# Two blocks on one core: the seven-product stage's weight places at 256 instead of 320 bytes, and `t2` ahead of `to` in the second attention's schedule

## The chip, the cores and the metric

One core of a Trainium2 chip. The time is the device time of one execution in microseconds (us), the median of three runs. Engines: PE (matmuls; PEld is its row of weight loads), DVE (vector), ACT (scalar), POOL, and SP, which here only issues DMAs.

## The reference, cut to what matters

A block with a mixer (a convolution branch and an attention with a forget gate) and a SwiGLU feed-forward, and then a differential attention layer; the last layer of the second block has no part in the result, since one layer of the list is run. All in fp32, with 512 tokens and width 1024.

```python
def swiglu(h, w_gate_up, w_down):
    gu = jnp.einsum("bsd,df->bsf", h, w_gate_up)     # 1024 x 5632
    g, u = jnp.split(gu, 2, axis=-1)
    return jnp.einsum("bsf,fd->bsd", jax.nn.silu(g) * u, w_down)

def diff_attention_layer(x, norm_g, w_in, ...):
    q, k, v, z = jnp.split(rms_norm(x, norm_g) @ w_in, 4, axis=-1)
    ...                                              # 16 heads, two maps of 64 each
    weights = probs[:, :, 0] - lam * probs[:, :, 1]
    o = einsum(weights, v)                           # causal, blocks of 128 queries
    o = rms_norm(o, head_norm_g) * (1.0 - lam_0)
    return x + (o.reshape(b, s, BRANCH) * jax.nn.silu(z)) @ w_out
```

## The kernel before

**Products in three parts.** Every fp32 operand x is kept as two fp32r tiles, high part and rest (`hth`/`htl` for the activations, `whi`/`wlo` for weights, `pth`/`ptl` for attention weights). ACT writes the high part by a copy (its helper `copy` is line 1291), DVE the rest by a subtraction (helper `lower`, line 1609). A product is three matmuls: high x high, high x rest, rest x high. The function `three` (lines 927 to 929, and 932 to 934 where weights are the stationary operand) writes them.

**One list of steps.** `Order` writes a list `STEPS` of named steps. Each engine walks the whole list and emits its own part of each step, so the order of the list is the order on PE, DVE, ACT and POOL alike; semaphores hold them together. `merge` deals out the steps of a projection of the next group (`proj2`) between those of the attention of the present pair of heads (`pair`), one `yield` at a time. `bank()` takes the next of four spare PSUM banks in turn, and PE's `claim` waits until the bank's last reader is done.

**The seven-product stage.** The gate and up projections (`gp` steps, blocks j = 1 to 10; block 0 is computed directly by `three`, steps `gu`) multiply 2 x 2 blocks by seven products instead of eight, with 256 tokens as moving operand. Each of the 70 products takes eight k-and-column pieces of three matmuls (L1162, L1164, L1165), 128 x 128 stationary by 256 columns. Their weights stand in four places of 1024 elements in `whi_all` and `wlo_all`, tiles of 4096 + 256 elements:

```python
SHIFT = 80                               # elements of 4 bytes
s = (first_slot + BLOCK(j, p)) % 4
c = SHIFT + 1024 * ((s + 2) % 4)
cs = slice(256 * kt + P * fb, 256 * kt + P * fb + P)   # inside the place; P = 128
```

The program puts `whi` at byte 44032 of a partition, `wlo` at 61440, and `hth`, `htl` and the other matmul operands of these stages also at multiples of 512. The weights of `three` start at multiples of 128 elements in these tiles, so on multiples of 512 bytes; those of the stage start 320 bytes past one. One further stationary operand is off that grid: `wf2`, which the step `fm` uses (L1014 and L1015, 16 columns of 4 bytes for each k from 0 to 7, 512 tokens moving), lies at byte 221152, which is 480 past a multiple of 512; its slice for k starts 64 k bytes further.

**The second attention's pair schedule.** For a pair of heads `even` and `odd`: `s2` computes scores, DVE takes maxima, ACT exponentials, `cb` combines the two maps, `t2` transposes the attention weights (three parts of up to four 128 x 128 tiles, L1230) and ACT and DVE copy them out as `pth2` and `ptl2` (shown as `pth` and `ptl`), `p2` multiplies them with v (L1243 to L1245, four key blocks, the third and fourth need part 2 of `t2`). `ga`/`gb` make the norm of a head. `to` transposes the gated norm of a head (L1261); DVE multiplies it with the head's result into `ots` (L1985), and ACT waits for that and sends `ots` to DRAM (L1585; for heads below 12), from where SP loads it back four heads at a time. POOL has no part in `to` or `t2`.

Of the kernel before, what the change touches and what calls it, by code (L numbers as in the profile page):

```python
# [172 lines left out]
class Order:  # L173
# [27 lines left out]
    def put(self, *step):  # L201
        self.steps.append(step)
# [42 lines left out]
    def bank(self):  # L245
        self.turns += 1
        return self.spare[self.turns % len(self.spare)]
# [312 lines left out]
    def pair(self, even):  # L560
        put, bank, odd, past = self.put, self.bank, even + 1, even > 0
        self.scores(even, 0)
        self.scores(even, 1)
        yield
        if past:
            put("t2", even - 1, 0, bank())
        put("cb", even, 0)
        put("ab", odd)
        yield
        if past:  # L570
            self.second_tiles(even - 1)
            put("t2", even - 1, 2, bank())
        put("cb", even, 1)
        yield
        self.scores(even, 2)
        self.scores(odd, 0)
        yield
        put("cb", even, 2)
        yield
        if past:  # L580
            put("to", even - 2, bank())
        put("cb", even, 3)
        yield
        put("cb", odd, 0)
        put("ab", odd + 1)
        yield
        if past:
            put("p2", even - 1, bank())
        put("cb", odd, 1)
        yield  # L590
        put("t2", even, 0, bank())
        yield
        self.second_tiles(even)
        yield
        self.scores(odd, 1)
        self.scores(odd, 2)
        yield
        if past:
            put("to", even - 1, bank())
        put("t2", even, 2, bank())  # L600
        put("cb", odd, 2)
        yield
        put("p2", even, bank())
        put("cb", odd, 3)
        yield
        yield
# [35 lines left out]
def build(nc, A, out, x1_d, x2_d, ot_d):  # L642
# [10 lines left out]
    with ExitStack() as ctx:  # L653
# [194 lines left out]
        BANK = lambda j, p: RING[(5 * (j - 1) + BANKS[p]) % 8]  # L848
        first_slot = 2 * (1 - H[W.mix + 1].slot)
        assert first_slot == 0  # L850
        SHIFT = 80
        p1_t, sg0_t, u2_t, u3_t, c22_t, c21_t = (tf[0][:, 0:512], tf[0][:, 512:1024], tf[1][:, 0:512],
                                                 tf[1][:, 512:1024], xf[0][:, 0:512], xf[0][:, 512:1024])
        moving = [(lambda k: (hth[:, k, 0:256], htl[:, k, 0:256])), (lambda k: (sh[2][:, k, :], sl[2][:, k, :])),
# [6 lines left out]
        def slot_of(j, p):  # L861
            s = (first_slot + BLOCK(j, p)) % 4
            c = SHIFT + 1024 * ((s + 2) % 4)
            cs = slice(c, c + 1024)
# [740 lines left out]
        def _(e):  # L1605
# [32 lines left out]
            for s in STEPS:  # L1638
# [234 lines left out]
                elif kind == "gx":  # L1873
                    j, p = a
                    o = ps[BANK(j, p)][:, :]
                    if p == 3:
                        dve.wait_ge(snap_a, j)
                        dve.wait_ge(mm, PRODUCT(j, 3))
                        e.tensor_tensor(u2_t, o, p1_t, ALU.add).then_inc(comb_d, 1)
                        dve.wait_ge(comb_d, COMB(j, U2))  # L1880
                        e.tensor_tensor(u3_t, ps[BANK(j, 1)][:, :], u2_t, ALU.add).then_inc(comb_d, 1)
                    elif p == 4:
                        dve.wait_ge(comb_d, COMB(j, U3))
                        dve.wait_ge(mm, PRODUCT(j, 4))
                        e.tensor_tensor(c22_t, o, u3_t, ALU.add).then_inc(comb_d, 1)
                    elif p == 5:
                        dve.wait_ge(mm, PRODUCT(j, 5))
                        e.tensor_tensor(c21_t, u3_t, o, ALU.subtract).then_inc(comb_d, 1)
                    elif p == 6:
                        dve.wait_ge(sg1_a, j)  # L1890
                        dve.wait_ge(comb_d, COMB(j, C22))
                        e.tensor_tensor(gu[:, 2 * j:2 * j + 2, 256:512], pair(c21_t), pair(c22_t),
                                        ALU.mult).then_inc(comb_d, 1)
                        dve.wait_ge(mm, PRODUCT(j, 6))
                        e.tensor_tensor(u2_t, o, u2_t, ALU.add).then_inc(comb_d, 1)
                        dve.wait_ge(comb_d, COMB(j, C12))
                        dve.wait_ge(sg0_a, j)
                        e.tensor_tensor(gu[:, 2 * j:2 * j + 2, 0:256], pair(sg0_t), pair(u2_t),
                                        ALU.mult).then_inc(comb_d, 1)
# [293 lines left out]
```

## Time and profile before

| | |
|---|---|
| median of 3 runs | 1282.76 us (1282.42 to 1284.1) |
| the profiled execution | 1282.49 us, of which the span from first to last instruction is 1280.8 us |
| PE busy | 1274.0 us of the span |
| DVE, ACT, POOL busy | 795.0, 611.6, 298.4 us |
| granted TensorE clock | 1.00 of 2.4 GHz over the whole span |
| seven-product stage | 392 to 590 us |
| second attention with its projections | about 729 to 1163 us |

In the views, a row has a start and a length in us, engine, line of the kernel, output and inputs. Matmuls are pipelined: their lengths overlap, and the pace is the distance between starts. Idle time in brackets is that of the row's engine ahead of it.

### The profile page before, as it was taken

The page shows a single profiled execution, that of the slowest core. Times are in us where ns is not written, and L with a number is a line of the kernel's source. Part 1 is how long each engine was busy: PE and PEld are TensorE (multiplying, and loading weights), DVE is VectorE, ACT ScalarE, POOL GpSimd, SP SyncE. Part 2 cuts the span into 40 slices and gives each one's busy share as a digit, 9 for nine tenths or more (in the row PEclk, how much of TensorE's full clock was granted, in tenths as well). Part 3 has the DMA queues.
Part 4 walks back from the last instruction along what each step waited for, and adds up shares of the span by engine and source line. Part 5 has one row for each costly group of instructions (what it writes and reads, how often), then busy time and mean ns, then how long its engine had stood idle before and what let it go on. Part 6 is the DMA issues. An engine that isn't in the chain of part 4 may idle for free.

```text
span 1280.8 us, 18355 instructions
## 1 busy us (share of the span) xinstructions
PE 1274.0 (99%) x7170; PEld 1085.6 (85%) x7170; DVE 795.0 (62%) x1578; ACT 611.6 (48%) x1300; POOL 298.4 (23%) x203
## 2 busy tenths in 40 slices
PE   9999999999999999999999999999999999999999
PEld 6788888888899999999888888888888888887787
DVE  5435665443479987877333647676767667677743
ACT  5336654333445444445233445565556555556531
POOL 2023310000055656540001412131312223131110
PEclk9999999999999999999999999999999999999999
DMA  6322232333533334243226322222222222223511
GB/s 235 108 58 75 59 99 71 96 98 99 205 124 105 105 121 132 67 132 115 82 99 218 112 66 84 82 74 74 83 71 98 88 75 75 74 81 123 184 59 66
DMA packets 110441, 130.35 MB, mean 102 GB/s; under 512 B 7569, under 2 KB 87697, under 8 KB 110354
## 3 DMA queue, kind: packets, MB, share of 16 engines
q1 hardware_dynamic: 104594, 112.39, 27.2%
q10 hardware_dynamic: 5760, 16.78, 3.6%
q8 instruction: 57, 0.93, 0.3%
q14 instruction: 30, 0.25, 0.1%
HBM read 119.72 MB, written 9.44 MB: 101 GB/s over the span
## 4 chain that ended last, share of the span: by engine, by line
PE 98%; DVE 1%; ACT 0%; DMA 0%; POOL 0%; issue 0%; SPq 0%; ACTq 0%
PE ps L927 17%; PE ps L929 16%; PE ps L928 16%; PE ps L932 7%; PE ps L934 7%; PE ps L933 7%; PE ps L1164 5%; PE ps L1165 5%; PE ps L1162 5%; PE ps L1220 3%; PE ps L1230 1%; PE ps L1202 1%; PE ps L1254 1%; PE ps L1244 1%; PE ps L1245 1%; PE ps L1243 1%
## 5 line engine op out<-in xcount | busy, mean ns | idle before, releaser
L1609 DVE TENSOR_TENSOR wlo<-raw,whi 128x512 fp32r<-128x512 f32 (+1 forms) x294 | 233.7, 821 | 187.2 <-ACT whi L1291 186.5
L1291 ACT ACTIVATE whi<-raw 128x512 fp32r<-128x512 f32 (+2 forms) x338 | 208.5, 649 | 117.9 <-PE ps L929 84.5
L927 PE MATMUL ps<-whi,hth 128*128 128x512 f32 x592 | 242.3, 409 | 0.2 <-DVE wlo L1609 0.2
L929 PE MATMUL ps<-wlo,hth 128*128 128x512 f32 x592 | 231.5, 391 | 0.0
L928 PE MATMUL ps<-whi,htl 128*128 128x512 f32 x592 | 231.2, 390 | 0.0
L2043 POOL TENSOR_TENSOR wlo<-raw,whi 128x384 fp32r<-128x384 f32 (+1 forms) x44 | 49.2, 1135 | 416.6 <-ACT whi L1291 416.6
L927 PEld LDWEIGHTS ps<-whi,hth 128*128 128x128 f32 x592 | 111.3, 188 | 26.4 <-issue 5.2
L929 PEld LDWEIGHTS ps<-wlo,hth 128*128 128x128 f32 x592 | 111.1, 188 | 24.7
L928 PEld LDWEIGHTS ps<-whi,htl 128*128 128x128 f32 x592 | 111.6, 188 | 19.2
L932 PE MATMUL ps<-hth,whi 128*128 128x512 f32 (+1 forms) x288 | 111.5, 387 | 0.0
L934 PE MATMUL ps<-hth,wlo 128*128 128x512 f32 (+1 forms) x288 | 108.9, 378 | 0.0
L933 PE MATMUL ps<-htl,whi 128*128 128x512 f32 (+1 forms) x288 | 108.9, 378 | 0.0
L1559 ACT ACTIVATE px<-px,nm 128x128 f32<-128x128 f32 (+3 forms) x128 | 70.4, 551 | 54.4 <-DVE nm L1949 54.4
L1165 PE MATMUL ps<-sh,wlo 128*128 128x256 f32 x320 | 89.9, 281 | 0.0
L1162 PE MATMUL ps<-sh,whi 128*128 128x256 f32 x320 | 89.9, 281 | 0.0
L1164 PE MATMUL ps<-sl,whi 128*128 128x256 f32 x320 | 89.9, 281 | 0.0
L2012 POOL TENSOR_TENSOR rq<-rq,neghalf 128x8 f32<-128x8 f32 x32 | 52.4, 1638 | 123.1 <-DVE rq L1912 123.1
L2102 POOL TENSOR_TENSOR hn<-hn,neghalf 128x4 f32<-128x4 f32 x16 | 16.8, 1051 | 247.5 <-DVE hn L1976 247.5
L1291 ACT ACTIVATE px<-px,rl 128x128 f32<-128x128 f32 (+1 forms) x64 | 36.0, 562 | 78.8 <-DVE rl L1962 78.8
L1609 DVE TENSOR_TENSOR wlo<-ts,whi 128x1024 fp32r<-128x1024 f32 x40 | 66.5, 1684 | 4.1 <-ACT whi L1291 4.1
L2081 POOL TENSOR_TENSOR ts<-raw 128x1024 f32<-128x1024 f32 x20 | 58.3, 2916 | 40.0 <-DVE wlo L1609 38.6
L1162 PE MATMUL ps<-hth,whi 128*128 128x256 f32 x240 | 67.4, 281 | 0.0
(362 smaller groups left out, 2913.9 us busy)
## 6 DMA issues: line engine op xcount, KB each, us to landing
raw<-in_l_w_in SPq DMA_DIRECT2D x64, 512.0 KB, 4.4
raw<-in_w_gate_up SPq DMA_DIRECT2D x44, 512.0 KB, 4.7
raw<-in_w_in SPq DMA_DIRECT2D x13, 1024.0 KB, 5.2
raw<-in_w_down SPq DMA_DIRECT2D x10, 1024.0 KB, 4.9
raw<-in_l_w_out SPq DMA_DIRECT2D x8, 1024.0 KB, 5.0
raw<-in_w_in SPq DMA_DIRECT2D x26, 256.0 KB, 3.5
raw<-in_w_branch SPq DMA_DIRECT2D x8, 512.0 KB, 3.9
raw<-in_w_out SPq DMA_DIRECT2D x4, 1024.0 KB, 4.9
```

The source lines that it names most:

```text
L927: e.matmul(o, ah, wh[:, cs], start=a, stop=False)
L928: e.matmul(o, al, wh[:, cs], start=False, stop=False)
L929: m = e.matmul(o, ah, wl[:, cs], start=False, stop=z)
L932: e.matmul(o, wh[:, cs], ah, start=a, stop=False)
L933: e.matmul(o, wh[:, cs], al, start=False, stop=False)
L934: m = e.matmul(o, wl[:, cs], ah, start=False, stop=z)
L1162: e.matmul(o, wh[:, cs], ah, start=q == 0 and kt == 0 and p not in (2, 6), stop=False, skip_group_check=True)
L1164: e.matmul(o, wh[:, cs], al, start=False, stop=False, skip_group_check=True)
L1165: m = e.matmul(o, wl[:, cs], ah, start=False, stop=z, skip_group_check=True)
L1291: return e.activation(out, in_, ACT.Copy, **how)
L1559: e.activation(sl, sl, ACT.Exp, bias=nm2[:, c:c + 1], scale=-1.0, accum_out=ls2[:, c:c + 1]).then_inc(exp2_a, 1)
L1609: return e.tensor_tensor(out, src, hi_part.bitcast(F32), ALU.subtract)
```

## The change

The weight places of the seven-product stage start at 64 elements (256 bytes) instead of 80 (320 bytes) past the start of the tile; sizes, order and waits stay as they are. In `pair`, for pairs after the first, the step `t2` (part 2 of head even) comes ahead of `to` (head even-1) in the list, on every engine; as `bank()` is called in the new order, the two also trade spare banks. For the first pair nothing changes.

```diff
@@ pair
         self.scores(odd, 2)
         yield
         if past:
+            put("t2", even, 2, bank())
             put("to", even - 1, bank())
-        put("t2", even, 2, bank())
+        else:
+            put("t2", even, 2, bank())
         put("cb", odd, 2)
         yield
         put("p2", even, bank())
@@ build
-        SHIFT = 80
+        SHIFT = 64
```

## Rows read from the trace of the kernel before

**Rows 1.** The page's busy line, and the table by stage (seven products; second attention).

```profile
PE 1274.0 (99%) x7170; PEld 1085.6 (85%) x7170; DVE 795.0 (62%) x1578; ACT 611.6 (48%) x1300; POOL 298.4 (23%) x203
...
core 0: us, PE busy (x) PEld busy (x) DVE busy (x) ACT busy (x) POOL busy (x), PEclk, DMA share, GB/s
392.00:590.00 198.00, 198.00 (x1684) 198.00 (x1683) 164.96 (x146) 92.36 (x106) 108.03 (x37) 1.00 0.34 107
729.00:1163.00 434.00, 433.98 (x2334) 357.40 (x2334) 295.74 (x781) 245.40 (x617) 99.63 (x70) 1.00 0.24 80
```

**Rows 2.** PE's waits from 20 us on, with total, times and longest.

```profile
PE ps L1243 <- DVE ptl L1609: 0.9, 1, 0.9
```

**Rows 3.** Weight loads by line: duration min/median/max in ns, first and last start.

```profile
L1162 PEld LDWEIGHTS ps<-sh,whi x320: 192/192/192, 395.0 to 589.6; 128*128 128x128 f32 x160
...
L1164 PEld LDWEIGHTS ps<-sl,whi x320: 187/188/188, 395.1 to 589.8; 128*128 128x128 f32 x160
...
L933 PEld LDWEIGHTS ps<-htl,whi x18: 192/192/192, 380.0 to 391.9; 128*128 128x128 f32 x18
```

**Rows 4.** Timeline of PE at the stage's start: start, length, instruction.

```profile
391.53 0.28 PE L932 MATMUL ps<-hth,whi 128*128 128x256 f32 x1
...
391.89 0.28 PE L932 MATMUL ps<-hth,whi 128*128 128x256 f32 x1
...
392.25 0.28 PE L1162 MATMUL ps<-hth,whi 128*128 128x256 f32 x1
```

**Rows 5.** Timeline of PE, the last L1162 of 560.

```profile
589.76 0.28 PE L1162 MATMUL ps<-sh,whi 128*128 128x256 f32 x1
```

**Rows 6.** Timeline of PE, `fm`: k = 0, 1, 2, and the matmul after its last.

```profile
59.17 0.39 PE L1014 MATMUL ps<-hth,wf 128*16 128x512 f32 x1
...
59.62 0.40 PE L1014 MATMUL ps<-hth,wf 128*16 128x512 f32 x1
...
60.09 0.39 PE L1014 MATMUL ps<-hth,wf 128*16 128x512 f32 x1
...
62.85 0.39 PE L932 MATMUL ps<-hth,whi 128*128 128x512 f32 x1
```

**Rows 7.** Timeline of the last pair's step with `to` and `t2`, PE and ACT.

```profile
1160.44 0.60 PE L1261 MATMUL ps<-ident,og 128*128 128x128 f32 x4
...
1160.88 0.49 PE L1230 MATMUL ps<-ident,px 128*128 128x128 f32 x3
...
1162.72 0.36 ACT L1551 ACTIVATE zs<-ps 128x256 f32<-128x256 f32 x1
```

**Rows 8.** Timeline of PE, the last pair's `p2` of head 12, and what follows.

```profile
1163.93 0.39 PE L1243 MATMUL ps<-pth,v2h 128*128 128x512 f32 x1
...
1166.21 0.39 PE L1243 MATMUL ps<-pth,v2h 128*128 128x256 f32 x1 [0.92 <-DVE ptl L1609]
...
1166.85 0.28 PE L1245 MATMUL ps<-ptl,v2h 128*128 128x128 f32 x1
1166.96 0.45 PE L927 MATMUL ps<-whi,hth 128*128 128x512 f32 x1
```

**Rows 9.** The chain that ended last, there: start, length, what.

```profile
1163.69 0.33 DVE zs L1934
...
1164.71 0.33 ACTq L1585
...
1165.08 0.50 ACT pth L1291
...
1165.60 0.57 DVE ptl L1609
```

**Rows 10.** Timeline of PE, an undisturbed `p2`: first and third block, and what follows.

```profile
1142.01 0.39 PE L1243 MATMUL ps<-pth,v2h 128*128 128x512 f32 x1
...
1143.21 0.29 PE L1243 MATMUL ps<-pth,v2h 128*128 128x256 f32 x1
...
1143.87 0.44 PE L927 MATMUL ps<-whi,hth 128*128 128x512 f32 x1
```

**Rows 11.** Timeline of SP's queue: the read-back of heads 8 to 11.

```profile
1169.01 0.37 SPq L2127 DMA_DIRECT2D raw<-ot_dram  x1
```

## The prediction

> **What bounds the kernel now.** First the busy line of the page and the table by stage [rows 1]: PE is busy 1274.0 of 1280.8 us, the granted clock is 1.00 (the 2.4 GHz level) in both big stages, and DVE, ACT and the DMAs have room. So the span is the number of matmuls times their pace, and an edit is worth something only if it changes a pace or one of the few waits of PE. Then the list of PE's waits: after the first 20 us PE waited once for another engine, 0.9 us for `ptl` [rows 2]. Busy time hides the pace, though: a 256-column matmul lasts 0.28 us [rows 4], yet 1680 of them fit into 198 us. The pace is the distance between starts, so the timeline of PE comes next.
>
> **Part one, the place.** L1162, L1164 and L1165 run 560 times each. L1162 starts first at 392.25 and last at 589.76 [rows 4, 5]; with 559 steps between, three matmuls take 353.3 ns, 117.8 each. The lines in front of them (L932 to L934, the directly computed product, also 256 columns and the same kind of moving tile) start a new three at 391.53, 391.89 and 392.25: 360 ns, 120 each [rows 4]. What differs is the stationary operand. In `three` each begins on a multiple of 512 bytes; in the stage it begins 320 bytes past one. Its loads differ too: 192 ns on all of L933, 187 to 188 on L1164 [rows 3], and on L1165 the same as on L1164. The aligned three and the shifted three touch at 392.25, with clock and neighbours unchanged, so I take the place as the cause of the 2.2 ns a matmul. The shift is worth 560 x (360 - 353.3) = 3.7 us today.
>
> What does a place 256 bytes past such a multiple do? No row of before has one. Modulo 512, 256 is as far from 0 as can be; modulo 256, 128 or 64 it is the aligned place again, while 320 is not (modulo 128 it is 64). One stretch can tell the readings apart. In `fm` (L1014, L1015) the stationary operand is 16 columns wide and moves on by 64 bytes with k, from 480 modulo 512. L1014's matmul takes 0.39 us for each of the four even k (places 480, 96, 224, 352) and 0.40 us for each of the four odd k (32, 160, 288, 416) [rows 6] (the first three of eight stand there). There the time goes with the place modulo 128, and the 128 and 256 bits make no difference. The moving tiles alternate with k as well and could be the cause, though the same tiles under 512-column matmuls elsewhere (L932) don't alternate. One stretch at other widths is a hint, no proof.
>
> I cost the edit from it: 256 behaves as 0, and the pace goes back to 120 ns, **+3.7 us**. Below, the bound is 128-column matmuls, which follow each other at 0.11 us (1166.85 to 1166.96) [rows 8]: 330 ns for three, 560 x 23.3 = 13 us saved. Above, the slow places of `fm`: its 16 matmuls take 62.85 - 59.17 = 3.68 us [rows 6], 230 ns each; if the fast ones take the 226 ns of 59.17 to 59.62, the slow ones take some 234, 8 ns more. Laid on top of 120 ns that is 1680 x 10 = 17 us lost. I take neither end, because the aligned rows have the very shape of the ones changed.
>
> Nothing else hangs on the place. ACT and DVE write the same sizes, each block after the product of the block that held its place; the last place ends 64 bytes earlier. Should their writes take longer, they have cover: ACT is busy 92.4 and DVE 165.0 of the 198 us [rows 1]; without cover 5% more on DVE would be 8 us.
>
> **Part two, the schedule.** Each of the six pairs after the first does, in one step, `to` of head even-1 and then `t2` of head even, part 2. On PE that is four transposes and three in one burst [rows 7], without a gap; trading them changes nothing there. The lists of ACT and DVE are what matters, for they follow the same order. ACT reaches `to` first, where it waits for DVE's `ots` (L1985) before it sends the head, and only then copies `pth`; DVE makes `ots` first and `ptl` last. The chain of waits shows it in the last pair [rows 9]: DVE is done with `zs` at 1164.02, `ots` fills the time to the DMA issue at 1164.71, `pth` is copied from 1165.08, `ptl` made from 1165.60 to 1166.17, and L1243 starts at 1166.21 [rows 8]. In an undisturbed call L1243 starts on its third block 1.20 us after the call's first matmul [rows 10], so PE wanted it at 1163.93 + 1.20 = 1165.13. The call takes 1166.96 - 1163.93 = 3.03 us against 1143.87 - 1142.01 = 1.86 [rows 8, 10]: 1.17 us lost.
>
> After the trade ACT is free at 1163.08 (L1551, 1162.72 + 0.36), the transposes long done [rows 7]; `pth` takes 0.50 [rows 9] and ends at 1163.6. DVE is free at 1164.02 and `ptl` takes 0.57 [rows 9]: 1164.6. PE wants it at 1165.13, so the wait goes with half a microsecond to spare: **-1.17 us**. The other five pairs show no wait of PE for `ptl` [rows 2], so they give nothing.
>
> What is late next? `ots` comes one `ptl` later, about 0.6 us, and with it ACT's send. The send of head 11 goes out at 1164.71 today [rows 9]; its read-back on SP is issued at 1169.01 [rows 11], 4.3 us later, so 0.6 us is covered. Without that cover SP's load would come 0.6 us later, and the loads queued behind it. Behind the send on ACT stand `cb`'s copies of `px`, which wait for DVE's reciprocals; those stand behind `ots` and `ptl` on DVE, in sum the same work without ACT's turn in the middle, so they come earlier. `p2`'s copies wait for PE. POOL's list holds neither step. The traded banks: `t2` takes the bank that `to` had, and the other way round; each is claimed again by the next pair's first `s2`, several microseconds behind both. If the cover failed in all six pairs, the loss would be 6 x 1.17 = 7 us; I see no mechanism for it.
>
> **Sum.** The profiled execution took 1282.49 us (span 1280.8, and 1.7 around it): 1282.49 + 3.7 - 1.2 = 1285.0. The median of the runs shown is 0.3 us above that execution, so against it the forecast is **1285.3 us**, 0.20% more. About 0.2% (2.6 us) is what a measurement of this kernel can tell from no change; the forecast stands on that edge.
>
> **Rivals.**
> A. The place 256 keeps what 320 gives: any place off the 512 grid will do. For it: all aligned rows share that grid. Against it: [rows 6]. Time 1282.76 - 1.2 = 1281.6, on the faster side of before. It decides if three starts still take 353 ns, and the stage then ends where it does now.
> The Trainium skill, SBUF — State Buffer, Specifications (TRN2), names 16-byte cachelines, with a penalty for each cross to a new one, as the unit that an access pays by. 0, 256 and 320 are all multiples of 16, so by it no pace moves and the time is this rival's; the trace already disagrees, by the 2.2 ns between places 0 and 320.
> B. 256 is better than 320. For it: today L1162's load still shows the aligned 192 ns where L1164's shows 188 [rows 3], so one of three has something left. Against it: no row of another place shows it. If that one gained as the others did, 3.3 ns in three, the stage saves 560 x 3.3 = 1.9 us, in all 1279.7; at twice that 1277.8; at the bound 1268.6.
> C. 256 is worse than aligned, as the odd k of `fm`: from 1 ns a matmul (1.7 us on top, 1287.0) to the bound (1299).
> D. The schedule does not do what it says, since something else stands in front of `ptl` on DVE. Then 1.2 us are missing in any of these: 1286.5 for the forecast.
>
> **How the numbers follow.** The forecast has 0.48, A 0.25, B 0.18, C 0.09; D is a tenth within each. The range takes in the forecast with D's miss, A, and the nearer half of B: 1279.4 to 1286.6, which leaves out 0.18. The forecast's own range is 1284.6 to 1286.6. Faster by over 0.2% (below 1280.2) is most of B, 0.17. Slower by over 0.2% (above 1285.3) is C and under half of the forecast, 0.29. Within 0.2%: 0.54.
>
> **What would show it.** Part one: starts of three in the stage 360 ns apart, loads of 192 ns on L1164 and L1165, L1162's last start near 593.5 in place of 589.76. 353 ns is A, less is B. Part two: no wait of PE for `ptl`, `pth` copied before L1985 runs, and the last pair's call in 1.86 us. I am wrong if the place counts by bits that [rows 6] doesn't bear on, or if the trade delays a queue that I hold for covered.

## The result, and the profile after

The changed kernel takes 1285.53 us (median of 16 runs, 1284.75 to 1287.35) against 1282.83 for the kernel before (16 runs beside them): a ratio of 1.002, 95% interval 1.0013 to 1.0026. The forecast was 1285.3, its range 1279.4 to 1286.6. The profiled execution took 1285.92 us, with a span of 1284.2 against 1280.8.

The page's busy line, and the table of the stage (its span moved to 392.50 to 594.70):

```profile
PE 1277.9 (100%) x7170; PEld 1090.3 (85%) x7170; DVE 790.5 (62%) x1578; ACT 611.9 (48%) x1300; POOL 297.8 (23%) x203
...
392.50:594.70 202.20, 202.20 (x1687) 202.20 (x1687) 161.11 (x146) 92.71 (x106) 107.46 (x37) 1.00 0.34 106
```

The clock is the same 1.00; the stage is longer. The weight loads by line (minimum/median/maximum in ns), which answer to [rows 3]:

```profile
L1164 PEld LDWEIGHTS ps<-sh,whi x320: 192/192/192, 395.9 to 594.3; 128*128 128x128 f32 x160
...
L1166 PEld LDWEIGHTS ps<-sl,whi x320: 192/192/192, 396.0 to 594.4; 128*128 128x128 f32 x160
```

Lines of the kernel stand 2 lower than before. The timeline of PE at the stage's start and end, which answers to [rows 4, 5]:

```profile
392.43 0.28 PE L934 MATMUL ps<-hth,whi 128*128 128x256 f32 x1
...
392.79 0.28 PE L934 MATMUL ps<-hth,whi 128*128 128x256 f32 x1
...
393.15 0.28 PE L1164 MATMUL ps<-hth,whi 128*128 128x256 f32 x1
```

```profile
594.39 0.28 PE L1164 MATMUL ps<-sh,whi 128*128 128x256 f32 x1
```

L1164 starts first at 393.15, 0.36 after the last row of L934; the 559 steps to 594.39 are 360.0 ns each, and all loads are 192 ns (L1167's too). The aligned stretch and the stage are now alike.

The last pair, PE, ACT and DVE, with the queues of ACT and SP; it answers to [rows 7 to 9, 11]:

```profile
1164.85 0.49 PE L1232 MATMUL ps<-ident,px 128*128 128x128 f32 x3
...
1165.18 0.60 PE L1263 MATMUL ps<-ident,og 128*128 128x128 f32 x4
...
1167.13 0.36 ACT L1553 ACTIVATE zs<-ps 128x256 f32<-128x256 f32 x1
...
1167.40 0.47 ACT L1293 ACTIVATE pth<-ps 128x384 fp32r<-128x384 f32 x1
...
1168.02 0.41 DVE L1936 SCALAR_TENSOR_TENSOR zs<-zs,ps 128x256 f32<-128x256 f32 x1
...
1168.35 0.39 PE L1245 MATMUL ps<-pth,v2h 128*128 128x512 f32 x1
1168.35 0.55 DVE L1611 TENSOR_TENSOR ptl<-ps,pth 128x384 fp32r<-128x384 f32 x1
...
1168.82 0.74 DVE L1987 SCALAR_TENSOR_TENSOR ots<-oc,gh,ps 128x512 f32<-128x512 f32 x1
...
1169.55 0.29 PE L1245 MATMUL ps<-pth,v2h 128*128 128x256 f32 x1
1169.59 0.33 ACTq L1587 DMA_DIRECT2D ot_dram<-ots  x1
...
1170.20 0.44 PE L929 MATMUL ps<-whi,hth 128*128 128x512 f32 x1
```

```profile
1172.47 0.37 SPq L2129 DMA_DIRECT2D raw<-ot_dram  x1
```

`pth` is copied before `ots` exists, `ptl` is done at 1168.90, and L1245 wants it at 1169.55. The call of `p2` takes 1170.20 - 1168.35 = 1.85 us, and the list of PE's waits from 20 us on is empty.

Where the time went, by the starts of the same instruction in both traces, after minus before: 0.90 us at the stage's first matmul (393.15 - 392.25), 4.63 at the last L1164 (594.39 - 589.76), 4.42 at the last pair's `p2` (1168.35 - 1163.93), 3.24 behind it (1170.20 - 1166.96). So the stage cost 3.73 us, the attention up to the last pair gave 0.21, the last pair gave 1.18. The 0.90 us arose ahead of anything that the change touches, all of it before 13 us, and differs from trace to trace. Two things differ there: how long PE waits for its first operands, and when it leaves a slower pace. Its 128-column matmuls first start 213 ns apart and then 109 to 112. In the kernel before the step comes at 9.5 us; in the changed one 213 ns hold to 10.4 us, and the short steps follow from 11.4 us on. In `place_only`, a run below whose program is the same as before's up to the stage, even the 512-column matmuls start 427 ns apart until 15.0 us, and then 224 to 236. The row of the granted clock reads 1.00 through all of it, and no run shows what sets the moment.

### The profile page after: what moved, and what is told of

It reads as the page before. It is cut to its first block, busy times and chain, and to the rows that moved or that the text cites. A ratio compares the mean times of both kernels' runs of the same rounds, so it can differ in the third digit from the quotient of the medians.

```text
span 1284.2 us, 18355 instructions
## 1 busy us (share of the span) xinstructions
PE 1277.9 (100%) x7170; PEld 1090.3 (85%) x7170; DVE 790.5 (62%) x1578; ACT 611.9 (48%) x1300; POOL 297.8 (23%) x203
## 4 chain that ended last, share of the span: by engine, by line
PE 99%; DMA 1%; DVE 0%; ACT 0%; POOL 0%; SPq 0%; issue 0%
PE ps L929 17%; PE ps L931 16%; PE ps L930 16%; PE ps L934 7%; PE ps L935 7%; PE ps L936 7%; PE ps L1167 5%; PE ps L1166 5%; PE ps L1164 5%; PE ps L1222 3%; PE ps L1232 1%; PE ps L1204 1%; PE ps L1256 1%; PE ps L1247 1%; PE ps L1246 1%; PE ps L1245 1%
## 5 line engine op out<-in xcount | busy, mean ns | idle before, releaser
L1611 DVE TENSOR_TENSOR wlo<-raw,whi 128x512 fp32r<-128x512 f32 (+1 forms) x294 | 230.2, 809 | 190.2 <-ACT whi L1293 189.5
L934 PE MATMUL ps<-hth,whi 128*128 128x512 f32 (+1 forms) x288 | 111.5, 387 | 0.0
L1164 PE MATMUL ps<-sh,whi 128*128 128x256 f32 x320 | 90.6, 283 | 0.0
L1167 PE MATMUL ps<-sh,wlo 128*128 128x256 f32 x320 | 90.6, 283 | 0.0
L1164 PE MATMUL ps<-hth,whi 128*128 128x256 f32 x240 | 67.9, 283 | 0.0
L1166 PE MATMUL ps<-htl,whi 128*128 128x256 f32 x240 | 67.9, 283 | 0.0
```

Of the source, the lines that this page charges most:

```text
L934: e.matmul(o, wh[:, cs], ah, start=a, stop=False)
L1164: e.matmul(o, wh[:, cs], ah, start=q == 0 and kt == 0 and p not in (2, 6), stop=False, skip_group_check=True)
L1166: e.matmul(o, wh[:, cs], al, start=False, stop=False, skip_group_check=True)
L1167: m = e.matmul(o, wl[:, cs], ah, start=False, stop=z, skip_group_check=True)
L1611: return e.tensor_tensor(out, src, hi_part.bitcast(F32), ALU.subtract)
```

## The experiments

**The two parts alone.** `swap_only` is the new schedule with the old place; `place_only` the new place with the old schedule. Both were timed beside the kernel before, whose median there is 1282.95 us (15 runs).

```diff
 # swap_only, against the changed kernel
-        SHIFT = 64
+        SHIFT = 80
```

```diff
 # place_only, against the kernel before
-        SHIFT = 80
+        SHIFT = 64
```

> Only the schedule trade; the places stay at 320 bytes. Theory: three starts in the stage stay at 353.3 ns, PE's wait for ptl is gone, the last pair's call takes 1.86 us in place of 3.03, so 1.2 us less than before (1281.6). Rival (the trade costs something that the place hid, or gives nothing): 1282.8 or more. A first version that should beat both kernels.

> Only the place, 256 in place of 320 bytes; the old schedule. Theory: three starts at 360 ns, 3.7 us more than before (1286.5), and PE's wait for ptl stays as before. Rival (the two edits act on each other): the wait has another length than 0.9 us or the stage another pace than 360.

Measured: `swap_only` 1281.58 us (11 runs), ratio 0.999, interval 0.9981 to 0.9999, three matmuls in 353.33 ns, no wait of PE. `place_only` 1287.73 us (5 runs), ratio 1.0037, interval 1.0023 to 1.005, 360.00 ns, and PE's wait for `ptl` is there again:

```profile
PE ps L1243 <- DVE ptl L1609: 0.9, 1, 0.9
```

The parts have the signs and nearly the sizes of the forecast: -1.4 us measured for the schedule (1.2 forecast), +4.8 for the place (3.7). Of the +4.8, the stage in `place_only`'s own trace accounts for 3.7; its execution reached the stage 2.3 us later than before's, again from the start of the program. With 5 runs, the start is the likely rest, but that isn't shown. `swap_only` is the fastest of the four, 0.1% under the kernel before, with an interval that ends just below 1.

**Other places.** The new schedule with the places 16, 32, 48, 64 and 96 bytes past the grid (one number changed, `SHIFT` in 4-byte elements; one execution each, so the paces count here and not the times).

```diff
-        SHIFT = 64
+        SHIFT = 16        # sh16: 64 bytes; sh8: 32; sh24: 96; sh12: 48; sh4: 16
```

> Places at 64 bytes (16 elements) past a multiple of 512, new schedule. Rule modulo 128: 64 is what 320 is modulo 128, so 353.3 ns for three starts and 1281.6 us. Rule modulo 512 (only places far from the grid gain): 360 ns and 1285.5 us.

> Places at 32 bytes (8 elements), new schedule: 32 modulo 128, the slow class of the 16-column stretch. If that stretch speaks for this stage too: slower than aligned, some 127 ns a start (382 for three, 1298 us). If only the 64 bit counts: 360 ns for three, 1285.5. If any place off the grid does: 353 or less.

> Places at 96 bytes, with 96 modulo 128 the fast class of fm. By a rule with the 64 bit alone 353.3 ns; if 32-byte offsets gain by themselves as sh8 did (355.0), 355 or less. 360 would mean that 96 is aligned again.

> Places at 16 bytes. If any place off the 128-byte grid gains: 353 to 355 ns for three. If the unit is 32 bytes or more: 360.

> Places at 48 bytes, no pad. Between 32 bytes (355.0) and 64 (353.3): 353 to 355 ns if the gain grows with the distance up to 64. Less than 353 would be a place that beats both kernels.

| kernel | place, bytes | mean step of three matmuls, ns | median loads, ns | time, us |
|---|---|---|---|---|
| changed | 256 | 360.00 | 192 | 1285.53 |
| `sh4` | 16 | 355.00 | 188 | 1283.85 |
| `sh8` | 32 | 354.99 | 188 | 1282.68 |
| `sh12` | 48 | 355.00 | 190.5 | 1282.46 |
| `sh16` | 64 | 353.33 | 192, 188, 188 | 1281.47 |
| `sh24` | 96 | 355.35 | 188 | 1282.72 |
| `swap_only` | 320 | 353.33 | 192, 188, 188 | 1281.58 |

64 and 320 give the same pace and the same loads to the nanosecond, and so do 0 (the directly computed product) and 256. That rules out a count modulo 512, by which 64 and 320 would differ, and modulo 64, by which 320 would be 0. It doesn't tell 128 from 256, for no run put the places 128 or 192 bytes past the grid. But 32 and 96, which in `fm` stood 8 ns apart [rows 6], stand 0.1 ns a matmul apart here (354.99 and 355.35 for three, with one single step of 405 in the latter), and both are faster than 0. The slow class of `fm` doesn't carry over.

**Whose place?** A place of the stationary operand is also a distance to the moving one, whose tiles lie on the grid too. An unused tile moves what lies behind it. `pad_all` puts 64 bytes ahead of all these tiles (distance 0, own place 64 modulo 128). `pad_act` puts 64 bytes between the weights and the activations (distance 64, the weights' own place still 0 modulo 128). `pad32` and `pad96` do the latter with 32 and 96 bytes and set the place so that the stage's distance is again 64, at own places of 96 and 32.

```diff
 # pad_all: ahead of whi, pad_act: ahead of hth; both with SHIFT = 64
+        sbuf(ctx, "pad", [P, 16])
 # pad32: ahead of hth, with SHIFT = 24; pad96: [P, 24], with SHIFT = 8
+        sbuf(ctx, "pad", [P, 8])
```

> As the changed kernel (places at 256 bytes), with a pad of 64 bytes between the weight tiles and hth: weights stay at 0 modulo 128, hth, htl and every tile behind them move to 64 modulo 128. In the stage the stationary operand is at 0, the moving one at 64. If the distance between the two operands' places counts: 353.3 ns for three starts. If the stationary operand's own place counts: 360. In the projections (hth stationary, weights moving, 512 columns) the own-place theory allows a pace other than 227 ns, too.

> As the changed kernel, with the 64-byte pad ahead of whi: every matmul operand is at 64 modulo 128, the distance between stationary and moving is 0 as in the changed kernel. Own place: 353.3 ns for three. Distance: 360. In fm the slices of wf2 trade classes (even k at 32, odd k at 96): if the 0.40 us of odd k came from the place it goes to even k; if from the moving tile it stays with odd k.

> A pad of 32 bytes between the weight tiles and hth, places of the stage at 96 bytes, so that the stage has distance 64 (stationary place minus moving place, modulo 128). Distance theory: 353.3 ns for three in the stage. 512 columns: where hth is stationary (L929 to L931 of the changed kernel) the distance is 32, in fm the slow class: some 234 ns in place of 227; where the weights are stationary (L934 to L936) it is 96, the fast class: 227. Rival (only the stationary operand's own place counts): the stage at 96 gives 355.3, as in sh24.

> The pad is 96 bytes and the places at 32, so the stage has distance 64 again: 353.3 ns by distance, 355.0 by own place as in sh8. 512 columns: distances trade roles: hth stationary has 96, so 227 ns; weights stationary have 32, so 234. If neither is under 227 ns, distance 0 is already the best found for 512 columns.

Measured: `pad_all` 1286.02 us, three starts in 360.00 ns, all loads 192. `pad_act` 1298.2 us, mean of three 353.89 ns, with a wait of 0.4 us for DVE's `wlo` in it. `pad32` 1298.27 and 353.48; `pad96` 1302.59 and 353.47. The loads by line, `pad_all` first, then `pad_act`:

```profile
L1165 PEld LDWEIGHTS ps<-sh,whi x320: 192/192/192, 395.9 to 594.2; 128*128 128x128 f32 x160
```

```profile
L1165 PEld LDWEIGHTS ps<-sh,whi x320: 186/188/188, 399.8 to 594.9; 128*128 128x128 f32 x160
```

So an own place of 64 gives nothing without a distance, and a distance gives the faster pace without an own place: the prediction's quantity was the wrong one of two that coincide in this kernel. The direction makes no difference that these runs show: the weights lie 64 bytes past the moving operand in `sh16` and `pad32`, and 64 short of it, modulo 256, in `pad_act` and `pad96`. `fm` speaks against the own place too: in `pad_all` its operands moved by 64 bytes together, so that the even k stand where the odd ones stood, and the odd k kept their 0.40 us.

`pad_act`, `pad32` and `pad96` are slower all the same, by 12.7, 12.7 and 17.1 us against the changed kernel. The timeline of `pad_act`, 512-column matmuls near the end:

```profile
1168.21 0.39 PE L930 MATMUL ps<-whi,hth 128*128 128x512 f32 x1
1168.44 0.40 PE L931 MATMUL ps<-whi,htl 128*128 128x512 f32 x1
1168.68 0.39 PE L932 MATMUL ps<-wlo,hth 128*128 128x512 f32 x1
1168.91 0.40 PE L930 MATMUL ps<-whi,hth 128*128 128x512 f32 x1
```

And the same lines of the changed kernel (2 lower than before, 1 above the padded):

```profile
1166.31 0.39 PE L929 MATMUL ps<-whi,hth 128*128 128x512 f32 x1
1166.53 0.39 PE L930 MATMUL ps<-whi,htl 128*128 128x512 f32 x1
1166.76 0.39 PE L931 MATMUL ps<-wlo,hth 128*128 128x512 f32 x1
1166.99 0.39 PE L929 MATMUL ps<-whi,hth 128*128 128x512 f32 x1
```

Three take 0.70 us at a distance of 64 and 0.68 at 0, some 6.5 ns a matmul; on the same lines `pad32` and `pad96` show medians of 232 to 235 ns in place of 227, with single steps from 230 to 238. Both had been expected to have one fast and one slow class, 227 and 234 ns, by `fm`; neither distance is a fast one. The three lines run 592 times each on `hth` and `htl`. Summed from start to start of the next matmul they take 9.1 us more in `pad_act` than in `swap_only`, the same lines on `guh` and `gul` 3.2 us, and the 512-column lines with the weights stationary 1.0. That is 13.3 of the 16.4 us by which the two spans differ; another 2.1 us arise in the first 17 us of the program. For 512 columns the distance 0 is the fast one, for 256 columns the slow one. A place can be moved for the stage alone, as `SHIFT` does; the whole tile can't.

**Is it the place alone?** The intervals inside the padded stages are not 353.3 ns throughout. `pad_act` runs its first 31 threes at 340 ns (113.3 a matmul), then comes a wait of PE, and everything behind it is 353 or 354 (but for a single 400), with the same places. `pad32` and `pad96` hold 340 over a first stall, then lose it at a second. The last kernel keeps the old place and the new schedule and disturbs PE 20 times: ahead of products 0 and 3 of each of ten j it runs extra copies of the product's first matmul, which the real one overwrites, or waits for PE's own last product. In this kernel the moving operand is on the grid, as in `swap_only`.

```diff
 # kick, against swap_only, in the seven-product step, ahead of its matmuls
+                    if q == 0 and p in (0, 3):
+                        site = 2 * (j - 1) + p // 3
+                        kind_ = "abcdeadbecbdaecedcba"[site]
+                        ah0 = moving[p](0)[0]
+                        if kind_ == "d":
+                            e.wait_ge(mm, MM["gp", j, p, 0] - 1)
+                        else:
+                            for n_ in {"a": (128,), "b": (256,), "c": (64,), "e": (128, 128)}[kind_]:
+                                e.matmul(o[:, 0:n_], wh[:, 0:P], ah0[:, 0:n_], start=True, stop=False,
+                                         skip_group_check=True)
```

> The kernel with the old place (80 elements) and the new schedule, and in the seven-product stage, ahead of product 0 and of product 3 of each of the ten j, one small disturbance: one, two or a narrower extra copy of the product's first matmul (64, 128, 256 or two times 128 columns; the real one overwrites it), or a wait of TensorE for its own previous product. 20 sites in five kinds, four each. The operands' places are as with the old place alone. In the three kernels with a pad the stage ran at 340 ns per three matmuls up to a stall of TensorE and at 353.3 after one, with the same places before and after. Theory 'phase': places allow a set of steady paces, and which one runs is set by how the stream was entered. Then some sites are followed by 340 ns and others by 353.3, and the change comes at a disturbance and holds until the next. The extra work costs at most 20 x 0.4 = 8 us, and each product that runs at 340 gives back 8 x 13.3 = 0.11 us, 7.4 us if all 70 did. Rival 'place': 340 needs the moving operand off the 128-byte grid, as the pads made it, and something else ended it; then every product here stays at 353.3, and the run takes 1281.6 plus the extra work, 1283 to 1289 us.

Measured: 1281.86 us, with 20 more instructions and disturbances on PE than `swap_only`, which took 1281.95 in its profiled execution. The timeline of PE about the fifth site (kind e, j = 3), L1174 being the first of three; the four rows of the other pace come first:

```profile
430.73 0.28 PE L1174 MATMUL ps<-sh,whi 128*128 128x256 f32 x1
431.08 0.28 PE L1174 MATMUL ps<-sh,whi 128*128 128x256 f32 x1
431.44 0.28 PE L1174 MATMUL ps<-sh,whi 128*128 128x256 f32 x1
431.79 0.28 PE L1174 MATMUL ps<-sh,whi 128*128 128x256 f32 x1
432.14 0.33 PE L1168 MATMUL ps<-hth,whi 128*128 128x128 f32 x2
432.31 0.34 PE L1174 MATMUL ps<-hth,whi 128*128 128x256 f32 x1
...
433.07 0.28 PE L1174 MATMUL ps<-hth,whi 128*128 128x256 f32 x1
433.41 0.28 PE L1174 MATMUL ps<-hth,whi 128*128 128x256 f32 x1
433.75 0.28 PE L1174 MATMUL ps<-hth,whi 128*128 128x256 f32 x1
434.09 0.28 PE L1174 MATMUL ps<-hth,whi 128*128 128x256 f32 x1
```

Ahead of the two extra matmuls the starts lie 0.35 to 0.36 apart; from 433.07 on they lie 0.34 apart. That holds over product borders until the next disturbance. Read over all 70 products (8 threes each), 36 ran at 340 ns and 34 at 353.3:

| kind | sites | what followed |
|---|---|---|
| b, 256 columns more | 4 | the pace stayed as it was (2 at 340, 2 at 353.3) |
| a, 128 columns more | 4 | 340 to 353.3 twice, 353.3 to 340 once, 340 at the stage's start |
| d, wait for its own product | 4 | changed each time: twice up, twice down |
| c, 64 columns more | 4 | 340 to 353.3 twice, 353.3 to 340 once, stayed at 353.3 once |
| e, two of 128 | 4 | 340 each time, three of them from 353.3 |

One change, from 340 to 353.3, came without a disturbance of mine, at a three of 399 ns in j = 1. The theory of a phase stands and that of the place alone falls: with fixed places TensorE has two steady paces, and a disturbance can switch from one to the other. What in a disturbance decides isn't settled: b, d and e did the same at each of their four sites, a and c did not. The gain of 36 x 8 x 13.3 ns = 3.8 us paid for the 20 disturbances, about 0.2 us each: the stage's 559 steps take 353.6 ns in the mean, all included.

From these rows, an estimate that no run here tested: one disturbance of kind e at the stage's start and 340 ns to its end would save 560 x 13.3 ns = 7.5 us less some 0.3, 1274.4 us in place of `swap_only`'s 1281.6, if PE met no stall in the stage. The traces speak against that condition, so it is a bound. All four stages that ran 340 ns from their start (`pad_act`, `pad32`, `pad96`, `kick`) lost time between the fourth and the fifth product of j = 1; in `kick` that is the 399 ns. `pad32` and `pad96` then waited before the last product of j = 2. Here are PE's waits in the stage of `pad32`:

```profile
PE ps L1165 <- DVE xf L1888: 0.7, 1, 0.7
PE ps L1165 <- DVE wlo L1612: 0.2, 1, 0.2
```

Behind the wait for `xf` that product starts 36.72 us into the stage in `pad32` and 36.71 in `pad96`; `swap_only`, at 353.3 ns and without a wait, starts it at 36.75. Up to there the waits had taken back all that the faster pace had gained.

## Why the prediction was right

- **PE is the bound, and its pace is read from the distance of starts.** Shown: behind the first 13 us the span followed the pace and the one wait, and no other engine's.
- **The place costs 560 x 6.7 = +3.7 us.** 3.73 in the trace, and alone in `place_only` with the same 360.00 ns.
- **256 behaves as 0, because the place counts modulo 128.** Right in what it forecast, in part by luck, for the evidence of `fm` was weaker than its use. A count modulo 256 would have forecast the same, and no run here excludes it in the stage; modulo 64, which the working lists as a reading by which 320 is not aligned, was out from the start, as 320 is 5 x 64. The quantity is not the stationary operand's own place but its distance to the moving operand (`pad_all`, `pad_act`), and the order of classes in `fm` (32 slow, 96 fast) is not that of the stage. "I take the place as the cause" left out two things: the moving tiles' place, which I named only for `fm`, and the phase, which I didn't think of. The forecast survived, by luck, since neither changed here: the moving tiles stayed, and the stage ran in one phase from end to end, before and after. Why `fm` alternates stays open: distance fits `pad_all`, but no run separated it from k, and the distances 32 and 96 are both slow for 512 columns elsewhere (`pad32`, `pad96`).
- **Rival A and the Trainium skill's rule.** A's test was 353 ns, and it fell. The Trainium skill, SBUF — State Buffer, Specifications (TRN2), gives 16-byte cachelines as the unit of an access's cost. Here places that are all multiples of 16 gave 360, 355 and 353.3 ns, so the traces disagree. At `sh4`, one such line past the grid, most of the gain is there.
- **Rival B, something is left.** It had the wrong place for it (256 gave nothing), but the bound that I took from 128-column matmuls, 330 ns, was nearer to the truth than I held it: 340 was measured, though not at 256.
- **The schedule gives 1.17 us in the last pair.** 1.18; `ptl` came 0.65 us ahead of PE's need, with about 0.5 forecast. The order of `pth`, `ptl`, `ots` was the one worked out. `swap_only` confirms it alone.
- **The other five pairs give nothing.** They gave 0.2 us in sum, 20 to 54 ns each. PE had no wait for `ptl` there, but short gaps below what the list of waits shows; that the list is empty does not make a step free to the last 0.05 us.
- **What is late next is covered.** ACT's send came 1.24 us after `p2`'s start against 0.78, 0.46 later where I forecast 0.6; SP's read-back came 4.12 after it against 5.08, so it had moved with the shorter call all but 0.2 us. PE waited for none of it.
- **Sum.** 1282.49 + 3.7 - 1.2 = 1285.0 stands against 1285.92 in the profiled execution; the 0.9 us is the start of the program, which no step of mine priced. The medians are 2.7 apart, where 2.5 was forecast, so little of it is left in them.

## What to carry to other kernels

When PE is the bound, measure the distance between starts in a long run of equal matmuls, not their busy time, and list it step by step: two fixed values in one stage, 340 and 353.3 ns, were worth 3.8 us here in half of its products, and the schedule edit 1.2. Before moving an operand by some bytes, find out which shapes read it, for here the distance that helps 256 columns hurts 512, and test the distance and the own place apart with an unused tile. Moving a step within an in-order list is worth the idle time that the list makes ahead of the engine at the bound; here one undisturbed call gave it to 0.01 us. Before counting on a faster pace of that engine, see how far ahead of it the others are: at 340 ns PE met waits for DVE that it didn't meet at 353.3.

## What the runs showed of the hardware

- Matmuls of 128x256 with a new 128x128 load each follow each other at 120.0 ns when the stationary operand lies 0 or 256 bytes past the moving one (modulo 512), at 118.3 to 118.5 ns for 16, 32, 48 and 96, and at 117.8 or 113.3 for 64 (320 gave 117.8, and 113.3 in `kick`); 128 was not run. Of 512 columns, with activations stationary: 227 ns at 0, medians of 232 to 235 at 32, 64 and 96.
- At 64 and 320 the two paces are states that hold for hundreds of matmuls, over changes of tile and bank; some gaps and extra matmuls switched them and others didn't. None of the runs disturbed the stage at a distance of 0, but the aligned three of the directly computed product came back to 120.0 behind each block of transposes, after two threes of 357 at most.
- The start of this program, up to about 15 us, differs by up to 2.3 us between traces of the same code (before and `place_only`), with PE at 213 and then 110 ns for 128 columns at a granted clock of 1.00; a forecast below 0.2% has to be held against stretches of the trace, not the whole.
